# Decode units: the same steps behind other key tiles

## The reference

```
kv = (lat @ w_ukv).reshape(n_past + ds, MLA_HEADS, QK_NOPE_DIM + V_HEAD_DIM)
k_nope = rms_norm(kv[..., :QK_NOPE_DIM], k_nope_g)
...
sc = (jnp.einsum('qhd,khd->hqk', qn, k_nope)
      + jnp.einsum('qhd,kd->hqk', qr, kr)).astype(jnp.float32) * ATTN_SCALE
...
p = jax.nn.softmax(sc, axis=-1).astype(v.dtype)
return jnp.einsum('hqk,khd->qhd', p, v)
```

## Time and profile before

| what | us |
|---|---|
| median of 3 executions | 1078.58 (1077.5 to 1078.97) |
| the profiled execution | 1072.7 |
| its span, first to last instruction | 1070.9 |
| first and last key matmul (L1200) in it | 213.7, 589.0 |

### The profile page before, as it was taken

One profiled execution on the slowest core, in us unless ns is written; L12 is line 12 of the kernel. 1 busy time (PEld: TensorE's weight loads), 2 busy tenths in 40 slices (PEclk: granted clock), 3 DMA queues, 4 the chain that ended last, 5 costly groups with the idle time before them and its releaser, 6 DMA issues.

```text
span 1070.9 us, 20298 instructions
## 1 busy us (share of the span) xinstructions
PE 957.9 (89%) x7860; PEld 878.3 (82%) x7860; DVE 673.3 (63%) x1597; ACT 506.6 (47%) x839; POOL 179.9 (17%) x186
## 2 busy tenths in 40 slices
PE   5699986789889897989889697999999999999997
PEld 3388864478778787878778597999999999999997
DVE  3693055777777677677767455777777777742312
ACT  2324461477676676767666442444444443331210
POOL 0021330123222222332221013000000000100000
PEclk9699996899999999999999899999999999999999
DMA  9966734000202020202200353124324322544202
GB/s 341 298 202 197 236 134 164 1 1 20 80 21 80 21 80 21 99 27 73 80 2 10 90 139 53 40 79 112 84 78 110 86 78 78 149 122 112 58 4 80
DMA packets 106288, 100.11 MB, mean 93 GB/s; under 512 B 7119, under 2 KB 94943, under 8 KB 104126
## 3 DMA queue, kind: packets, MB, share of 16 engines
q1 hardware_dynamic: 102422, 77.91, 25.0%
q0 software_dynamic: 3456, 20.97, 5.5%
q10 hardware_dynamic: 340, 0.27, 0.1%
HBM read 96.41 MB, written 2.94 MB: 93 GB/s over the span
## 4 chain that ended last, share of the span: by engine, by line
PE 70%; DVE 12%; ACT 11%; issue 4%; DMA 2%; SPq 0%; POOL 0%; ACTq 0%; DVEq 0%
PE ps L843 46%; PE ps L1200 11%; PE ps L838 4%; DVE FS L2082 2%; DMA RW<-w_ada 2%; PE ps L1135 2%; PE ps L1112 2%; ACT krT L1547 2%; ACT RB L1547 2%; PE ps L869 1%; PE ps L1158 1%; ACT RB L1506 1%; ACT qrot L1547 1%; PE ps L1195 1%; DVE prep L2046 1%
## 5 line engine op out<-in xcount | busy, mean ns | idle before, releaser
L843 PE MATMUL ps<-normed_high,up_weights_high 128*128 128x260 f32 x704 | 142.7, 284 | 3.5 <-DVE normed_low L1764 3.3
L843 PE MATMUL ps<-normed_high,up_weights_low 128*128 128x260 f32 x704 | 142.4, 284 | 0.0
L843 PE MATMUL ps<-normed_low,up_weights_high 128*128 128x260 f32 x704 | 142.3, 284 | 0.0
L801 POOL TENSOR_TENSOR latents_low<-RB,latents_high 128x512 fp32r<-128x512 f32 (+1 forms) x72 | 87.5, 1215 | 270.3 <-ACT latents_high L1507 269.9
L1200 PE MATMUL ps<-key_weights_high,latents_high 128*128 128x260 f32 x528 | 123.7, 316 | 0.4 <-ACT latents_high L1507 0.4
L843 PEld LDWEIGHTS ps<-normed_high,up_weights_high 128*128 128x128 f32 x704 | 109.2, 190 | 4.0 <-issue 3.3
L1604 ACT ACTIVATE up_weights_high<-RW 128x1024 fp32r<-128x1024 f32 x44 | 46.6, 1061 | 136.0 <-PE ps L843 133.6
L843 PEld LDWEIGHTS ps<-normed_high,up_weights_low 128*128 128x128 f32 x704 | 109.2, 189 | 0.0
L843 PEld LDWEIGHTS ps<-normed_low,up_weights_high 128*128 128x128 f32 x704 | 108.9, 189 | 0.0
L1200 PE MATMUL ps<-key_weights_low,latents_high 128*128 128x260 f32 x528 | 106.3, 282 | 0.0
L1200 PE MATMUL ps<-key_weights_high,latents_low 128*128 128x260 f32 x528 | 106.3, 282 | 0.0
(11 more groups left out here) (315 smaller groups left out, 2109.3 us busy)
## 6 DMA issues: line engine op xcount, KB each, us to landing
RW<-w_ada SPq DMA_DIRECT2D x24, 1024.0 KB, 7.3
RW<-w_up SPq DMA_DIRECT2D x44, 512.0 KB, 4.9
RW<-w_down SPq DMA_DIRECT2D x8, 1408.0 KB, 7.0
RW<-w_in SPq DMA_DIRECT2D x11, 512.0 KB, 7.9
RB<-w_o SPq DMA_DIRECT2D x8, 512.0 KB, 4.0
RB<-x_prompt SPq DMA_DIRECT2D x2, 1024.0 KB, 12.8
o_y_p<-RB SPq DMA_DIRECT2D x4, 512.0 KB
cst<-consts SPq DMA_DIRECT2D x1, 845.0 KB, 11.0
```

Of the source, the lines that this page charges most:

```text
L801: nc.gpsimd.tensor_tensor(latL[:, g % 3, c:4 * P], turned[:, g % 3, c:4 * P], latH[:, g % 3, c:4 * P].bitcast(F32), ALU.subtract).then_inc ...
L843: last = mm(ps[j % 4][rows[0]:rows[1], h, 0:H], lhsT, src[:, h * H:(h + 1) * H], start=start, stop=stop)
```

## The change

No operation is added, removed or put on another engine. Steps are moved behind other tiles:

| step | engine | behind tile before | after |
|---|---|---|---|
| `turn_max` | TensorE | (1,1) | (1,2) |
| s20, `spread_max`, s3 | TensorE | (1,2), (2,0), (2,2) | (1,3), (2,1), (2,3) |
| p20, p3, p1, `head_mix` | TensorE | (3,1), (5,2), (6,0), (7,1) | (3,2), (5,3), (6,2), (7,2) |
| `rstd_keys` | ScalarE | (0,1) | (0,3) |
| `head_in` of qt, kt | ScalarE | (0,2), (0,3) | (0,1), (1,0) |
| `head_probs` s20, s3, s1 | ScalarE | (2,0), (3,1), (4,2) | (2,1), (3,2), (5,3) |
| `mixed` | ScalarE | (7,3) | (7,2) |
| `head_max`, `shift` | VectorE | (1,2), (2,1) | (1,0), (1,3) behind `row_max` of s20 |
| `row_max` s3 | VectorE | (3,0) | (2,3) |
| `norm_probs` s20, s3, s1 | VectorE | (2,3), (4,3), (5,1) | (2,1), (4,0), (5,3) |
| `turned_probs` p20, p3 | VectorE | (3,3), (5,3) | (3,2), (6,3) |
| `prob_sums`, `finish` | VectorE | (3,1), (5,0) | (3,3), (4,1) behind `row_max` of s1 |
| `split_queries` | VectorE | (6,3) | (7,1) |

The steps s1 and `pv` on TensorE, `probs` on ScalarE, and `scores_max`, `row_max` of s20 and s1 and `turned_probs` of p1 on VectorE stay. The helpers for the banks are rewritten to take the bank from the step's name, and the small columns of row maxima and sums are indexed by the block instead of by its place in the order; the order of uses of each bank is the same. `head_mix` waits for the release of p20 too, which stands before p3 in the same bank. The core of the diff (TensorE, then parts of ScalarE and VectorE):

```
-                        if (g, n) == (1, 1) and u > 0:
+                        if (g, n) == (1, 2) and u > 0:
                             turn_max(u)
-                        if (g, n) == (1, 2):
-                            head_scores(u, 1, "s20", (2, 0))
-                        if (g, n) == (2, 0) and u > 0:
+                        if (g, n) == (1, 3):
+                            head_scores(u, "s20", (2, 0))
+                        if (g, n) == (2, 1) and u > 0:
                             spread_max(u)
-                        if (g, n) == (2, 2):
-                            head_scores(u, 0, "s3", (3,))
...
+                        if (g, n) == (2, 3):
+                            head_scores(u, "s3", (3,))
...
-                        if (g, n) == (0, 1) and u > 0:
+                        if (g, n) == (0, 1):
+                            head_in(u, "qt", headq, QK)
+                        if (g, n) == (0, 3) and u > 0:
                             rstd_keys(u)
...
-                        if (g, n) == (1, 2) and u > 0:
+                        if (g, n) == (1, 0) and u > 0:
                             head_max(u)
                         if (g, n) == (1, 3):
-                            row_max(u, 1, "s20", (2, 0))
-                        if (g, n) == (2, 1) and u > 0:
+                            row_max(u, "s20", (2, 0))
+                        if (g, n) == (1, 3) and u > 0:
                             shift(u)
...
                         if (g, n) == (4, 1):
-                            row_max(u, 0, "s1", (1,))
...
+                            row_max(u, "s1", (1,))
+                        if (g, n) == (4, 1) and u > 0:
                             finish(u)
```

More of the change, by code:

```diff
@@ L218 @@
 KEY_JOBS = UNIT * NS
-BANKS = (("qt", "mt", "mb", "s3", "s1", "p1", "mix"), ("kt", "s20", "p20", "pv", "p3"))
+BANKS = (("qt", "mt", "mb", "s3", "s1", "p1", "mix"),
+         ("kt", "s20", "p20", "pv", "p3"))
+BANK = {name: b for b in range(2) for name in BANKS[b]}
 OF_FORMER = ("mt", "mb", "pv")
@@ L1081, in kclaim, with bclaim @@
                     pe.wait_ge(key_free[j % 3], j // 3)
-            def bclaim(b, name, u):
+            def bclaim(name, u):
+                b = BANK[name]
                 if BJ[b][name, u] == 0:
@@ L1122, in turn_probs @@
                     for a in range(n + 1):
-                        last = tr(bank(b)[:, at:at + P], hp[:, POFF[n] + P * a:POFF[n] + P * a + P], P)
+                        last = tr(bank(name)[:, at:at + P], hp[:, POFF[n] + P * a:POFF[n] + P * a + P], P)
                         at += P
-                last.then_inc(bank_full[b], 1)
+                last.then_inc(is_full(name), 1)
             def head_mix(u):
-                bclaim(0, "mix", u)
-                bfree(pe, 1, "p3", u)
-                bfree(pe, 0, "p1", u)
+                bclaim("mix", u)
+                bfree(pe, "p20", u)
+                bfree(pe, "p3", u)
+                bfree(pe, "p1", u)
                 pe.wait_ge(s_vtok, 4)
@@ L2092, in unit @@
                         if (g, n) == (2, 3):
-                            norm_probs(u, 1, "s20", (2, 0))
-                        if (g, n) == (3, 0):
-                            row_max(u, 0, "s3", (3,))
-                        if (g, n) == (3, 1) and u > 0:
+                            row_max(u, "s3", (3,))
+                        if (g, n) == (3, 2):
+                            turned_probs(u, "p20", (2, 0))
+                        if (g, n) == (3, 3) and u > 0:
                             prob_sums(u)
-                        if (g, n) == (3, 3):
-                            turned_probs(u, 1, "p20", (2, 0))
+                        if (g, n) == (4, 0):
+                            norm_probs(u, "s3", (3,))
@@ L2108, in unit @@
                         if (g, n) == (5, 3):
-                            turned_probs(u, 1, "p3", (3,))
+                            norm_probs(u, "s1", (1,))
                         if (g, n) == (6, 2):
-                            turned_probs(u, 0, "p1", (1,))
-                        if (g, n) == (6, 3) and u < NS - 1:
+                            turned_probs(u, "p1", (1,))
+                        if (g, n) == (6, 3):
+                            turned_probs(u, "p3", (3,))
+                        if (g, n) == (7, 1) and u < NS - 1:
```

192 lines of the change are left out of this document (95 added, 97 removed).

## The result

The changed kernel takes 1030.38 us (median of 4 executions, 1027.62 to 1031.46); the kernel before, run beside it, 1078.78 (1077.5 to 1083.32). The ratio is 0.954, with a 95% interval of 0.9506 to 0.9574: about 48.4 us faster.

What follows compares the result with a forecast made beforehand. TensorE, nearest to full, was taken as bound by its own work plus waits costing 8.0 us per unit. 38.4 for units 1 to 6, 3.7 and 6.6 make 48.7; 1078.6 - 48.7 = 1030 us, range 1021 to 1048.

Steps and rivals of the forecast that it cites:

- the sum: Eight units: 6.4 us less in each of units 1 to 6, 3.7 in unit 0, 6.6 in unit 7; 48.7 in all.
- The large wait: Group 2: s3 waits 2.57 us for late `shift`; with `shift` 4.0 earlier, the group loses 0.25 instead of 3.07.
- the walk: Following three engines through a unit in the new order: 1.5 of 8.0 us of waits left, 6.4 less per unit.
- the waits of group 3 and the one behind it: Groups 3 and 4, start to start: 0.4 us lost instead of 0.75, and 0 instead of 1.13.
- a first tile of group 3: It would wait 0.36 us, because `norm_probs` of s20 now holds the copy of (2,2).
- the 1 to 2 us that were given as a sign: Sign of being right: TensorE idle 1 to 2 us per unit instead of 6.17.
- The gathers: Issued 0.3 us behind `pv`, read in group 7; in time, with slack shrinking from 3.0 to 2.3 us.
- the waits only move: Rival: new waits replace old ones, 3 us per unit stay and the gain is 23; 1055 us, chance 0.12.
- slots are the limit: Rival: TensorE's waits come from too few slots, so order cannot remove them; no change, 1078.6 us, chance 0.02.
- The ring through `pv`: Rival: late `prob_sums` delays `pv` while `finish` holds the copies of (4,2) and (4,3); slower, 1086 us, chance 0.04.
- The tail: Behind the last unit: a chain of single steps keeping its length; a longer one was a sign of being wrong.
- the 5.9 us between profile and median: Kernel before: the median lies 5.9 us above the profiled 1072.7; this was taken to be outside of the units.

Runs made afterwards that it cites:

- b_shift: Kernel before with only `shift` moved on VectorE, from behind tile (2,1) to directly behind `row_max` of s20 at (1,3); 1066.6 us, ratio 0.9812.
- b_probs: Kernel before with only `head_probs` of s20 moved one tile later on ScalarE, from behind (2,0) to behind (2,1); ratio 0.9925.
- a_shift_back: Changed kernel with only `shift` put back behind (2,1) on VectorE; 1030.85 us, ratio 0.9475 to the kernel before.
- b_first_half: Kernel before with only the moves up to group 2 and `row_max` of s3; 1035.59 us, ratio 0.9592.
- b_start: Kernel before with only ScalarE's start order of the changed kernel (`rstd_keys`, `head_in` of qt and kt); ratio 1.0026.
- before_again: Kernel before, unchanged, profiled a second time; that profiled execution took 1086.04 us.
- b_second_half: Kernel before with only the rest of the moves, groups 3 to 8 without `row_max` of s3; 1071.53 us, ratio 0.9905.

## Why the prediction was right, and where not

**The time.** 1030 us was predicted, 1030.38 measured, and the terms of the sum hold: units 1 to 6 lost 6.33 each on average (6.4), unit 0 3.80 (3.7), unit 7 6.60 (6.6); together 48.4 us by the units' own lengths, 48.1 by the first and last key matmul, for the 48.7 of the sum.

**The large wait.** Right in place, cause and size. b_shift and b_probs each move one link of the chain alone, and the wait shrinks by 2.33 and 0.90, where 2.3 and 1.0 were expected; `shift` came 3.9 us earlier (4.0). By a_shift_back, though, the new place of `shift` itself isn't what the change hangs on.

**The walk by groups.** From transposes to transposes groups 1 to 4 now take 5.81, 5.23, 4.30 and 6.49; the walk had 5.64, 5.05, 4.53 and 6.40. The sum (21.83 for 21.62) is better than its parts. One step was put down wrongly: for the waits of group 3 and the one behind it the walk goes through `norm_probs` of s20, p20, `prob_sums` and `finish`, and `row_max` of s3 isn't in it. b_first_half shows that 1.5 of the 1.8 us go when p20, `prob_sums` and `finish` stay, and by the rows there it is `row_max` of s3 that had held both copies. The walk also kept 0.36 us for a first tile of group 3 behind `norm_probs`; after the change no such wait is listed. `finish` waited 0.29 for `pv` (0.1 predicted), at no cost that shows. TensorE's idle time, 0.52, is below the 1 to 2 us that were given as a sign, while the time left by the count from start to start, 8.0 - 6.33 = 1.7, is near the 1.5 of the walk.

**The gathers.** In time. Behind `pv` the first is issued at 362.15:

```profile
362.15 0.98 POOL L770 DMA_INDIRECT RW<-cache_kv_latent,half_of  x1 [2.63 <-PE ps L1168]
```

It landed at 367.95 by the trace, and the transposes that read it start at 370.28: 2.3 us of slack, as predicted. No transposes wait for one in unit 3.

**The rivals.** That the waits only move fell: 0.52 us of idle time per unit is left. That slots are the limit fell too: of the three slot waits, two went in b_first_half and the third, 0.38, is 0.18 (0.17 in b_start, so by ScalarE's start order), with the same three slots. So here the repeating gap that the Trainium skill (Perfetto Trace Analysis, Optimization Strategy) takes for a possible lack of buffers wasn't one. The ring through `pv` didn't close.

**What was wrong.** The tail was to keep its length, and a longer one was named as a sign of being wrong: it took 4.7 us more in the profile, with a half-speed stretch twice as long. Nothing in it is shown to come from the change, since the kernel before has the same tail in its second profile. And the 5.9 us between profile and median, "I take that to be outside of the units": before_again puts 6.1 of its 13.3 us inside of them, as falls of the clock around the wait for s3. So the first profile was the kernel before near its best (its lowest time on record is 1072.28), and the change wins 48 us of waits and, as far as eight profiles without a fall tell, those falls too. That sum and median agree to 0.4 us is partly luck: against the profile alone the sum gives 1072.7 - 48.7 = 1024.0, and the profile after took 7.5 more (4.7 in the tail, 2.1 ahead of the units, 0.6 in them), which the 5.9 happened to make up for.

## What to carry to other kernels

When engines with in-order queues share a few buffers, look at the longest wait first, and ask not what the instruction that ends it costs but what that one stands behind on its own engine: moving one step two tiles ahead took 2.3 of 6.2 idle us per unit. Waits one group later, which looked like a lack of buffers, were of the same kind, but they had a step of their own: they stayed in b_shift and went in b_first_half. Count such waits from start to start, since a part of their cost isn't listed as idle time, but don't take all of it for winnable: 1.7 of the 8.0 us stayed, and two tries at them won 0.15 and 0.22. Expect the parts not to add up: `shift` was worth 2.3 us alone and 0.4 as the last part. Profile the kernel before twice ahead of building on the difference between its profile and its median.

## What the hardware showed

**The clock falls around waits of a few us.** In the fourteen profiles of this case TensorE's granted clock fell to half within the key stretch 19 times (half-speed stretches that began before it aren't counted), each time between 0.7 us ahead and 1.7 us behind the end of a wait of 1.65 us or more. The six profiles with waits over 1 us had 0, 4, 1, 3, 5 and 6 falls (before, before_again, b_shift, b_probs, b_start, b_second_half); the eight without had none in their 64 units. The same wait often goes without a fall: none of the seven of 2.57 in the first profile of before had one. What decides it wasn't tried. The Trainium skill (TensorE: Matmul & The Clock Gate, Part 1: The HAM clock gate) says that the clock goes back to half after idle time; the rows agree in kind.

**One VectorE instruction took six times its time beside a GpSimd one.** In two units of b_shift a 128x8 step of `scores_max` (L2000) took 1.33 us instead of 0.23, ending when GpSimd's `low_latents` ended, and `turn_max` waited 2.52 instead of 1.44. The rows of units 5 and 4:

```profile
446.72 1.33 DVE L2000 TENSOR_SCALAR RB<-RB,cst 128x8 f32<-128x8 f32 x1
446.77 1.26 POOL L801 TENSOR_TENSOR latents_low<-RB,latents_high 128x512 fp32r<-128x512 f32 x1 [3.20 <-ACT latents_high L1507]
...
401.27 0.23 DVE L2000 TENSOR_SCALAR RB<-RB,cst 128x8 f32<-128x8 f32 x1
401.32 1.30 POOL L801 TENSOR_TENSOR latents_low<-RB,latents_high 128x512 fp32r<-128x512 f32 x1 [2.99 <-ACT latents_high L1507]
```

Both pairs start 0.05 us apart; what makes the difference wasn't tried. It isn't rare: in both profiles of the kernel before and in the four variants that leave `split_queries` behind (6,3), its second step (L2035) takes 1.1 us in unit 1 instead of 0.17, again until `low_latents` ends, and group 6 of that unit is 0.2 longer than in the others. In the seven profiles of the changed kernel and its variants no VectorE instruction of the key stretch is over 0.3 us longer than the median of its kind.
